# Merged attention with keys and queries stored in the order of reading, queries in a ring per unit, all values resident and four key groups in the ring

## The reference

```python
def diff_attend_prompt(q, k, v, lam):          # 1024 tokens, per head two sub-heads of 64, values of 128
    s = einsum('bqhcd,bkhcd->bhcqk', qi, k) * scale      # causal mask, blocks of 128 queries
    a = softmax(s)
    w = a[:, :, 0] - lam * a[:, :, 1]
    return einsum('bhqk,bkhv->bqhv', w, v)
def diff_attend_sample(q, k, v, lam, k_past, v_past):    # 8 sequences, 32 pages each
    s = concat(q . k_past, q . k (masked)) * scale
    a = softmax(s)
    w = a[:, :, 0] - lam * a[:, :, 1]
    return einsum(w[..., :P], v_past) + einsum(w[..., P:], v)
```

## Time and profile before

| | us |
|---|---|
| median of 3 executions | 2063.23 (2060.85 to 2072.15) |
| profiled execution | 2071.64 |
| its span | 2070.0 |
| TensorE busy | 1876.4 (91%) |
| VectorE busy | 977.5 (47%) |
| ScalarE busy | 609.0 (29%) |
| GpSimd busy | 399.9 (19%) |

### The profile page before, as it was taken

One profiled execution on the slowest core, in us unless ns is written; L12 is line 12 of the kernel. 1 busy time (PEld: TensorE's weight loads), 2 busy tenths in 40 slices (PEclk: granted clock), 3 DMA queues, 4 the chain that ended last, 5 costly groups with the idle time before them and its releaser, 6 DMA issues. The chain is left out here.

```text
span 2070.0 us, 35207 instructions
## 1 busy us (share of the span) xinstructions
PE 1876.4 (91%) x13412; PEld 1723.4 (83%) x13412; DVE 977.5 (47%) x1356; ACT 609.0 (29%) x1086; POOL 399.9 (19%) x393
## 2 busy tenths in 40 slices
PE   4999999566799898996899999999999999999898
PEld 4999999453466666664898999999999999998798
DVE  4224720486577676775334343334343333436543
ACT  4113321432465554554232111111111111113320
POOL 1112320341123233334112011011101101104210
PEclk9999999696899999999899999999999999999899
DMA  4333530204899999996311111111111111110221
GB/s 138 96 84 85 161 95 20 64 3 122 263 311 327 335 316 333 314 314 201 111 46 47 41 50 43 42 52 31 51 42 51 41 42 52 31 52 21 84 63 44
DMA packets 195486, 239.03 MB, mean 115 GB/s; under 512 B 13425, under 2 KB 136258, under 8 KB 195330
## 3 DMA queue, kind: packets, MB, share of 16 engines
q1 hardware_dynamic: 174850, 169.76, 26.9%
q0 software_dynamic: 20480, 67.13, 9.9%
HBM read 215.44 MB, written 16.92 MB: 112 GB/s over the span
## 5 line engine op out<-in xcount | busy, mean ns | idle before, releaser
L150 PE MATMUL psum<-h_hi,w_hi 128*128 128x364 f32 x1248 | 279.1, 332 | 1.7 <-issue 1.7
L150 PE MATMUL psum<-h_lo,w_hi 128*128 128x364 f32 x1248 | 276.8, 331 | 0.0
L150 PE MATMUL psum<-h_hi,w_lo 128*128 128x364 f32 x1248 | 275.4, 329 | 0.0
L2070 ACT ACTIVATE w_hi<-w_raw 128x1024 fp32r<-128x1024 f32 x66 | 68.8, 1059 | 583.7 <-PE psum L150 564.4
L150 PEld LDWEIGHTS psum<-h_hi,w_hi 128*128 128x128 f32 x1248 | 215.6, 189 | 3.9 <-issue 3.1
L150 PEld LDWEIGHTS psum<-h_lo,w_hi 128*128 128x128 f32 x1248 | 217.7, 189 | 0.0
L150 PEld LDWEIGHTS psum<-h_hi,w_lo 128*128 128x128 f32 x1248 | 216.8, 189 | 0.0
L2046 POOL TENSOR_TENSOR w_raw<-w_raw,gains 128x1024 f32<-128x1024 f32 x42 | 84.9, 2022 | 645.0 <-DMA w_raw<-in_w_ffn_gate 356.4
L1154 POOL DMA_DIRECT2D dec_v<-in_cache_v x256 | 137.5, 537 | 347.5 <-issue 346.9
L150 PE MATMUL psum<-x_hi,w_hi 128*128 128x364 f32 x792 | 188.8, 347 | 10.5 <-DVE x_lo L1903 6.6
L150 PE MATMUL psum<-x_hi,w_lo 128*128 128x364 f32 x792 | 176.6, 332 | 0.0
(11 more groups left out here) (262 smaller groups left out, 2798.5 us busy)
## 6 DMA issues: line engine op xcount, KB each, us to landing
dec_k<-in_cache_k SPq DMA_DIRECT2D x256, 256.0 KB, 5.3
dec_v<-in_cache_v POOLq DMA_DIRECT2D x256, 256.0 KB, 5.2
w_raw<-in_w_in SPq DMA_DIRECT2D x25, 512.0 KB, 3.9
w_raw<-in_w_ffn_gate SPq DMA_DIRECT2D x22, 512.0 KB, 3.8
w_raw<-in_w_ffn_up SPq DMA_DIRECT2D x22, 512.0 KB, 3.8
w_raw<-in_w_ffn_down SPq DMA_DIRECT2D x22, 512.0 KB, 4.3
feat_swap<-feat_n SPq DMA_DIRECT2D x32, 136.5 KB, 2.4
x_in<-in_x_prompt SPq DMA_DIRECT2D x4, 1024.0 KB, 8.2
```

Source lines behind the costliest of these rows:

```text
L150: ins = pe.matmul(out[:, c, 0:SPAN], w(k), x(k)[:, c * SPAN:c * SPAN + SPAN], start=n == 0 and w is whi and x is xhi, stop=n == len(ks) - ...
L2070: act.activation(m.whi[:, slot], m.raw[:, u], ACT.Copy).then_inc(s["w_hi"], 1)
```

## The change

- The scratch for keys is laid out as it is read: per head, for even and odd key blocks apart; that for queries per head and query block. The new tokens' parts get scratch of their own (`kS`, `qS`). A tile is stored with three DMAs instead of one.
- A head's keys are loaded in four parts of 128 rows' halves with long rows (`load_keys`), two sets of buffers as before. Queries are loaded per unit into a ring of four (`load_queries`, two DMAs of 64 KB). The values of all heads are loaded once, at the end of linear attention.
- The key ring has four slots; three groups are loaded in the phase before (`PRE`), the fourth at the start of the attention.
- In SP's loop the pages come first, then parts of keys and queries.
- `m.wt` has one buffer.
- ScalarE takes the turned keys of head 1, and copies the first piece of weights, ahead of the prompt's exponentials. VectorE combines a unit after it has copied turned keys and probabilities.

```diff
@@ input projection, SP
-                    sp.dma_start(scr["kT"][t - 8] if t < 12 else scr["qT"][t - 12], m.rot[:, t % 2, :]
-                                 ).then_inc(qk_stored[t % 2], 16)
+                    h = (t - 8) % 4
+                    for c in range(2):
+                        if t < 12:
+                            dst = scr["kT"][h, c].rearrange("p (b n) -> p b n", n=P)
+                            src = m.rot[:, t % 2, 0:NP].rearrange("p (b two n) -> p b two n", two=2, n=P)[:, :, c, :]
+                        else:
+                            dst = scr["qT"][h, :, :, c, :].rearrange("i d n -> d i n")
+                            src = m.rot[DK * c:DK * c + DK, t % 2, 0:NP].rearrange("p (i n) -> p i n", n=P)
+                        sp.dma_start(dst, src).then_inc(qk_stored[t % 2], 16)
+                    sp.dma_start(scr["kS" if t < 12 else "qS"][h], m.rot[:, t % 2, NP:NP + NS]).then_inc(qk_stored[t % 2], 16)
@@ linear attention, SP
-            for n in range(KR):
+            for n in range(PRE):
                 load_pages(sp, m, io["cache_k"], m.kr, n, pages_in, n)
-            for part in range(HEAD_PARTS):
-                load_head(sp, io, m, scr, 0, part, head_in, head_in)
+            for part in range(4):
+                load_keys(sp, m, scr, 0, part, head_in)
+            for n in range(QR):
+                load_queries(sp, m, scr, n, head_in)
+            sp.dma_start(m.av[:, :, :], io["new_v_prompt"].rearrange("(c p) f -> p c f", p=P)).then_inc(head_in, 16)
@@ sizes and loads
-KR, VR = 3, 4
+KR, VR, QR, PRE = 4, 4, 4, 3
+def load_keys(eng, m, scr, h, part, sem):
+    c, r = divmod(part, 2)
+    eng.dma_start(m.ak[h % 2][DK * r:DK * r + DK, c, :], scr["kT"][h, r, DK * c:DK * c + DK, :]).then_inc(sem, 16)
+def load_queries(eng, m, scr, n, sem):
+    h, i = UNITS[n]
+    for r in range(2):
+        eng.dma_start(m.aq[DK * r:DK * r + DK, n % QR], scr["qT"][h, i]).then_inc(sem, 16)
@@ attention, SP
+            for n in range(PRE, KR):
+                load_pages(sp, m, io["cache_k"], m.kr, n, k_page_in[n], n)
             sp.dma_start(m.vs[0:NS, :], io["new_v_sample"]).then_inc(d["new_v_in"], 16)
-            first_of = {1: KR, 2: 22, 3: 38}
+            first_of = {1: KR, 2: KR + 17, 3: KR + 33}
             for n in range(KR, NKV):
+                sp.wait_ge(d["ring_filled"], ring.filled(("keys", n - KR, H - 1)))
+                load_pages(sp, m, io["cache_k"], m.kr, n % KR, k_page_in[n % KR], n)
                 for h, first in first_of.items():
-                    if first <= n < first + HEAD_PARTS:
+                    if first <= n < first + 4:
                         if h >= 2 and n == first:
                             sp.wait_ge(s["scored"], 2 * 8 * (h - 1))
-                            sp.wait_ge(s["o_done"], 8 * (h - 1))
-                        load_head(sp, io, m, scr, h, n - first, qk_in[h], v_in[h])
-                sp.wait_ge(d["ring_filled"], ring.filled(("keys", n - KR, H - 1)))
-                load_pages(sp, m, io["cache_k"], m.kr, n % KR, k_page_in[n % KR], n)
+                        load_keys(sp, m, scr, h, n - first, k_in[h])
+                unit = n // 2 + 1
+                if n % 2 == 0 and QR <= unit < NU:
+                    sp.wait_ge(s["scored"], 2 * (unit - QR) + 2)
+                    load_queries(sp, m, scr, unit, q_in[unit % QR])
@@ attention, ScalarE
-                if n >= 2:
-                    act.wait_ge(s["o_done"], n - 1)
-                act.activation(m.wt[:, u, a:b], W_BANK[:, 0:b - a], ACT.Copy).then_inc(s["wt_copied"], 1)
+                if n >= 1:
+                    act.wait_ge(s["o_done"], n)
+                act.activation(m.wt[:, a:b], W_BANK[:, 0:b - a], ACT.Copy).then_inc(s["wt_copied"], 1)
...
                 if t < NKV:
                     take_keys(t, 0)
+                    take_keys(t, 1)
+                if c == 1 and 0 <= n - 1 < NU:
+                    copy_weights(n - 1, 0)
                 prompt_exps(t - 1)
-                if t < NKV:
-                    take_keys(t, 1)
                 if first_group:
                     exps(v)
                 if c == 0 and 0 <= n - 2 < NU:
                     copy_out(n - 2)
-                if c == 1 and 0 <= n - 1 < NU:
-                    copy_weights(n - 1, 0)
@@ attention, TensorE
+                if c == 0 and n >= QR:
+                    pe.wait_ge(q_in[n % QR], 32 * (n // QR))
-                    ins = pe.matmul(score_banks[:, r, 0:shown(i) * P], m.aq[u][rows, c, i * P:i * P + P],
+                    ins = pe.matmul(score_banks[:, r, 0:shown(i) * P], m.aq[rows, n % QR, c, :],
...
-                    ins = pe.matmul(W_BANK[:, 0:DV], m.wt[:, u, b * P:b * P + P], m.av[h % 2][:, b, :],
+                    ins = pe.matmul(W_BANK[:, 0:DV], m.wt[:, b * P:b * P + P], m.av[:, b, h * DV:h * DV + DV],
@@ attention, VectorE
-                if c == 0 and 0 <= n - 1 < NU:
-                    prompt_combine(n - 1)
                 if t < NKV:
                     take_keys(t, 3)
                 if 0 <= v < NKV:
                     if v % NG == 0:
                         take_new_p(v // NG)
                     take_p(v)
+                if c == 0 and 0 <= n - 1 < NU:
+                    prompt_combine(n - 1)
                 prompt_maxima(t)
```

More of the change, by code:

```diff
@@ L298, in _ @@
                 sp.wait_ge(stored[u], 32 * 6)
-                sp.wait_ge(qk_stored[u], 16 * 4)
+                sp.wait_ge(qk_stored[u], 48 * 4)
         @block.gpsimd
@@ L321, in _ @@
                     if t >= 10:
-                        gp.wait_ge(qk_stored[u], 16 * ((t - 8) // 2))
+                        gp.wait_ge(qk_stored[u], 48 * ((t - 8) // 2))
                         if t - 2 < 12:
@@ L660, in _ @@
             sp.wait_ge(s["stored"], 64)
-            sp.wait_ge(pages_in, 64 * KR)
-            sp.wait_ge(head_in, 16 * HEAD_PARTS)
+            sp.wait_ge(pages_in, 64 * PRE)
+            sp.wait_ge(head_in, 16 * (4 + 2 * QR + 1))
         @block.gpsimd
@@ L1046, in attention_memory @@
     m.ap, o = m.at("att_p", o, [P, 2, 2, NP])
-    m.wt, o = m.at("att_wt", o, [P, 2, NP])
+    m.wt, o = m.at("att_wt", o, [P, NP])
     ak1, o = m.at("att_k1", o, [P, 2, NP // 2])
-    av1, o = m.at("att_v1", o, [P, TT - 1, DV])
+    m.pts, o = m.at("dec_pt", o, [P, 2, 4, P])
+    m.pg, o = m.at("dec_p", o, [P, 2, 4 * PAGE])
     assert o == O_RB, o
-    aq0, o = m.at("att_q0", o, [P, 2, NP])
+    m.av, o = m.at("att_v", o, [P, TT - 1, H * DV])
+    m.vs, o = m.at("dec_new_v", o, [P, H * DV])
     ak0, o = m.at("att_k0", o, [P, 2, NP // 2])
-    av0, o = m.at("att_v0", o, [P, TT - 1, DV])
-    aq1, o = m.at("att_q1", o, [P, 2, NP])
-    m.aq, m.ak, m.av = (aq0, aq1), (ak0, ak1), (av0, av1)
+    m.aq, o = m.at("att_q", o, [P, QR, 2, P])
+    m.ak = (ak0, ak1)
     m.kr, o = m.at("dec_k", o, [P, KR, 4, H * P])
     m.vr, o = m.at("dec_v", o, [P, VR, 4, H * P])
-    m.vs, o = m.at("dec_new_v", o, [P, H * DV])
-    m.pts, o = m.at("dec_pt", o, [P, 2, 4, P])
-    m.pg, o = m.at("dec_p", o, [P, 2, 4 * PAGE])
     m.kts, o = m.at("dec_new_k", o, [P, H, NS])
     m.qs, o = m.at("dec_q", o, [P, H, NS])
+    m.ptn, o = m.at("dec_ptn", o, [P, P])
+    m.sc, o = m.at("att_small", o, [P, 80])
     m.osc, o = m.at("dec_osc", o, [P, DV])
     m.lamp, o = m.at("lam_prod", o, [P, 2, DK])
-    m.ptn, o = m.at("dec_ptn", o, [P, P])
-    m.sc, o = m.at("att_small", o, [P, 80])
     assert o <= O_U + 4 * TB, o
@@ L1191, in attention @@
     d = {n: sems("p4_" + n) for n in names.split()}
-    qk_in = [sems(f"p3_qk_in{h}") for h in range(H)]
-    v_in = [sems(f"p3_v_in{h}") for h in range(H)]
+    k_in = [sems(f"p3_k_in{h}") for h in range(H)]
+    q_in = [sems(f"p3_q_in{r}") for r in range(QR)]
     k_page_in = [sems(f"p4_k_in{r}") for r in range(KR)]
@@ L1231, in _ @@
         def _(sp):
[L1232 to L1233 removed]
+            sp.dma_start(m.qs[:, :, :], scr["qS"].rearrange("h p t -> p h t")).then_inc(d["new_in"], 16)
+            sp.dma_start(m.kts[:, :, :], scr["kS"].rearrange("h p t -> p h t")).then_inc(d["new_in"], 16)
             sp.dma_start(m.lam[:, :, :], io["lam_params"].broadcast_to([P, 4, DK])).then_inc(s["lam_in"], 16)
+            for n in range(PRE, KR):
+                load_pages(sp, m, io["cache_k"], m.kr, n, k_page_in[n], n)
             sp.dma_start(m.vs[0:NS, :], io["new_v_sample"]).then_inc(d["new_v_in"], 16)
[L1236 removed]
+            first_of = {1: KR, 2: KR + 17, 3: KR + 33}
             for n in range(KR, NKV):
+                sp.wait_ge(d["ring_filled"], ring.filled(("keys", n - KR, H - 1)))
+                load_pages(sp, m, io["cache_k"], m.kr, n % KR, k_page_in[n % KR], n)
                 for h, first in first_of.items():
[L1239 removed]
+                    if first <= n < first + 4:
                         if h >= 2 and n == first:
                             sp.wait_ge(s["scored"], 2 * 8 * (h - 1))
[L1242 to L1245 removed]
+                        load_keys(sp, m, scr, h, n - first, k_in[h])
```

(18 more changed lines are left out.)

## The result

| | before | after |
|---|---|---|
| median | 2063.81 us (2060.85 to 2072.15, 4 executions) | 2039.31 us (2036.58 to 2041.59, 4 executions) |
| profiled execution | 2071.64 us | 2040.47 us |
| its span | 2070.0 us | 2038.8 us |
| TensorE busy | 1876.4 us | 1863.9 us |

The ratio of the times is 0.9874 with a 95% interval of 0.9843 to 0.9906: 24.5 us less on the medians, 31.2 us between the two profiled executions.

A forecast was written before the change was run, and what follows sets the result against it. TensorE was taken to bound an attention step, with transfers mattering only where late. The terms -13 - 7 - 10 + 4 = -26 us, taken from 2063.2 us, gave 2037 us, with a range of 2026 to 2056.

The forecast's parts named there:

- The bound of a step: Merged attention: TensorE bounds a step, 6.49 us undisturbed (103.8 us for sixteen); transfers matter only where they are late.
- Head loads: Attention, heads 2 and 3: lighter loads and a fourth key slot remove all stalls, -13 us, bounds -13.1 and 0.
- Start: Attention steps 3 to 9: earlier key groups and fewer head parts ahead, -7 us, bounds -9.9 and -4.
- Order: Attention, ScalarE and VectorE reordered: TensorE waits less for copies, 9 us and 1 us, together -10, bounds 0 and -19.
- the walk: Attention step 52: the second key copy goes first, scores start at 868.2 instead of 868.8, 0.6 of 0.83 us kept.
- Residue: Attention: key and value groups still late at the faster pace, +4 us, bounds 0 and +11.
- The rival in which transfers become the bound: Attention: the queues move 128 MB at 327 GB/s, only -15 us, 2048 us; chance 0.20.
- Costs at nothing: Projection stores, first loads in linear attention, single weights' buffer: covered, no cost; value-page waits of 8.0 us stay.
- Signs: Attention: sixteen steps near 101 us, key-page waits under 5, line 1452's under 7, no 1.2 GHz clock between 550 and 900.
- Slower rival: Attention, VectorE: the combination behind the probabilities' copy exceeds its 1.2 us cover, transposes wait, +15 us, 2078 us; chance 0.06.

The follow-up runs named there:

- e6_act_order_only: The changed kernel with VectorE's old order (combination ahead of the key copy) and ScalarE's new one; 2054.85 us, ratio 0.9952.

## Why the prediction was right, point by point

Forecast 2037 us, range 2026 to 2056, faster by over 0.5%; measured 2039.3.

- **The bound of a step.** Right: the undisturbed step is set by TensorE and what it waits for on ScalarE and VectorE. With the old order and the new loads it is 103.8 us for sixteen, three times.
- **Head loads, -13.** In the pair of profiled executions it is exact (13.1 to 0). But the term was taken from one execution, and the second profile of the same program had 7.5 us there. As a term for the medians it was too large by several us. The bounds held. One of the three slow clocks in it I read wrongly: the one at 791.4 us follows no long key wait (1.2 us, 4.8 us earlier) but a 1.6 us wait for ScalarE in step 41, the kind of step that meets a slow clock without head loads too (below). The mechanism was half right: neither the values in the stage nor the 512-byte pieces make keys late; the kernel with both back and four slots has 100.1 to 100.2 us. What is left is the queries' transfers, their size or their crowding into nine steps, or the issue of parts ahead of the pages; the fourth slot is worth some 6.5 us beside it.
- **Start, -7.** 6.3 us in the first profile, with no wait for pages at all; the two us I set aside for late pages did not come, but there were 3.7 us of waits of the prompt scores for exponentials (0.6 before), and the slow clock at the start of the stage lasted 13.7 us where it was 10.2. The steps 0 to 8 take 44.9 to 47.0 us in the kernels with the new loads and order, and 44.8 with the new loads and the old order, so this gain is the loads'.
- **Order, -10.** 12.1 us, 3.7 in sixteen steps instead of 3.0. At step 52 the walk was right to a tenth: 0.6 us for the scores, and the step fell by 1.1 us. What I mis-sized is VectorE's share: I gave ScalarE nine tenths of it, but its order without VectorE's loses the whole. I had followed the combination behind its new place, and never asked what it would do in the old one once the exponentials come later. That the 8.8 us at line 1446 would stay was wrong too: they fell to 5.8; the 6.1 us before the key transposes were in no term.
- **Residue, +4.** Did not exist. I took 327 GB/s at a share of 1.05 for what the queues can give with head parts. The kernel with old pieces and values per head and four slots carried 356 GB/s at the same share of 1.05. The rival in which transfers become the bound, built on 327 GB/s, falls with it. The Trainium skill's figure of about 358 GB/s (DMA: Bandwidth & Descriptors, Specifications) agrees with the 350 to 359 GB/s over sixteen steps of full clock in the kernels with four slots and the new order; the 389 GB/s of rows 5 over 3.4 us lie above it. The same page of the Trainium skill (Bandwidth) lists 138 GB/s for a transfer of 64 KB, by which the queries would have cost some 14 us more; that did not show. The 64 query loads of 64 KB land in 5.3 us (median) while the queues carry 350 to 354 GB/s.
- **Costs at nothing.** All held: projection and linear attention within 1 us, no wait for the single weights' buffer, value waits behind the last key group 8.7 us for 8.0. The stores of a tile take SP some 2.0 us to issue instead of 0.6, inside the 8 us of cover.
- **Signs.** The stretches, the key waits and line 1452's successor came as written. "No granted clock of 1.2 GHz between 550 and 900" held in the first profile of the changed kernel and not in its second (570.0 and 621.2 us).
- **Slower rival.** A combination that makes others wait exists, but in the old place and not in the new one: ahead of the copies it waits for the later exponentials and makes the copy of the probabilities behind it late (`e6_act_order_only`). Behind them its 1.2 us of cover were enough.

The sum of -26 met the median's -24.5 partly by luck, since two errors cancelled: the stalls' term was too large for the median, the residue too large the other way. Split by ratios, the loads bring 0.0079, some 16 us (the terms were -13 - 7 + 4 = -16), and the order on top of them some 10.

## What to carry to other kernels

A stall that comes from late transfers is a draw, not a constant: take its size from two executions, and the size of an undisturbed step from repeated equal stretches, which here agree within 0.2%. When work is moved behind other work on one engine, ask for each engine that waits for the moved work what is queued behind that wait; here ScalarE's reordering paid only with VectorE's; VectorE's alone was not tried. And a rate at which the queues happened to be busy is not the rate that they can give.

## What the runs showed of the hardware

The granted clock of TensorE fell to 1.2 GHz for 3.4 us without a long wait before it. In the changed kernel no wait in steps 9 to 60 is longer than 1.0 us, and yet step 17 ran at 0.82 in one profile and at 1.00 in the other, for 1.6 us. In the nine profiles of kernels with the new loads and four slots, old pieces and other orders included, it fell 13 times in steps 9 to 62: three kept the full clock throughout, six did not. Each time it was in a step that begins a new sequence, and the longest wait just before was 1.6 us. In the changed kernel TensorE is busy 6.2 of the 8.1 us of step 17. The kernel with the weights' copy behind met it four times in its one profile and lost more there than its order had gained. The Trainium skill (TensorE: Matmul & The Clock Gate, HAM oscillation) tells of a clock that falls in TensorE's waits for a DMA; in step 17 of the changed kernel TensorE waits for ScalarE and VectorE only, and no more than 1.0 us at a time. Why one execution meets it and another does not stays open.

A share of the DMA engines of 1.05 came with 327 GB/s in the kernel before (640 to 700 us) and with 356 GB/s in one with the same keys and values but other queries, order of issue and number of slots (585.7 to 685.9 us). The share does not say how much is still to be had.
